# Where the stationary tiles of a two-block float32 kernel begin in SBUF

## What is computed

```python
proj = x @ w_in                                   # (256, 2048) @ (2048, ...)
merged = g_a * (o_a @ w_o_dsa) + g_b * (o_b @ w_o_moba)
x = layer_norm(ALPHA * x + merged @ w_out, ...)
x = layer_norm(ALPHA * x + mem_attention(x @ w_q, mem @ w_kv) @ w_o, ...)
g, u = jnp.split(x @ w_ffn_in, 2, axis=-1)
x = layer_norm(ALPHA * x + (silu(g) * u) @ w_ffn_out, ...)
# second block
proj = rmsnorm(x) @ w_in_2                        # three branches and their gates
y = x + sum(gates * (ys @ w_up_2)) @ w_out_2
```

## Time and profile before

| | |
|---|---|
| median of 3 runs | 2322.28 us (2319.61 to 2326.85) |
| profiled execution, span | 2323.2 us |
| PE busy | 2262.6 us, 97% |
| PEld busy (weight loads) | 1852.2 us, 80% |
| DVE busy | 1305.4 us, 56% |
| ACT busy | 1044.2 us, 45% |
| POOL busy | 167.2 us, 7% |
| read from and written to HBM | 421 MB over DMA, 181 GB/s |
| mean granted TensorE clock | 0.990 |

### The profile page before, as it was taken

One profiled execution on the slowest core, in us unless ns is written; L12 is line 12 of the kernel. 1 busy time (PEld: TensorE's weight loads), 2 busy tenths in 40 slices (PEclk: granted clock), 3 DMA queues, 4 the chain that ended last, 5 costly groups with the idle time before them and its releaser, 6 DMA issues.

```text
span 2323.2 us, 30087 instructions
## 1 busy us (share of the span) xinstructions
PE 2262.6 (97%) x10167; PEld 1852.2 (80%) x10167; DVE 1305.4 (56%) x1571; ACT 1044.2 (45%) x1243; POOL 167.2 (7%) x175
## 2 busy tenths in 40 slices
PE   7999999999999899999999999998999999999999
PEld 6777888888877678878887888776888788888887
DVE  5444655566567665445444444456655565645664
ACT  4443444555434444433444334334445444545643
POOL 1000000001204040000000000004000000200020
PEclk9999999999999999999999999998999999999999
DMA  7655554555855455555665556554556655655555
GB/s 214 205 162 155 170 169 153 180 156 180 272 195 164 156 181 187 178 187 184 195 190 181 181 181 199 176 176 137 177 167 202 191 177 185 208 176 183 175 181 164
DMA packets 216427, 421.11 MB, mean 181 GB/s; under 512 B 15225, under 2 KB 19361, under 8 KB 214433
## 3 DMA queue, kind: packets, MB, share of 16 engines
q1 hardware_dynamic: 213184, 402.31, 55.2%
q0 software_dynamic: 3168, 17.82, 2.2%
HBM read 417.97 MB, written 2.11 MB: 181 GB/s over the span
## 4 chain that ended last, share of the span: by engine, by line
PE 94%; DVE 3%; DMA 1%; ACT 1%; issue 1%; SPq 0%; DVEq 0%; ACTq 0%
PE b_ps L532 88%; PE b_ps L574 1%; PE b_ps L557 1%; PE b_ps L614 1%; DVE b_x_res L1452 1%; PE b_ps L676 1%; DVE b_w_lo L1294 1%; DVE b_x_res L1443 1%; DMA b_stage<-in_w_up 1%; PE b_ps L629 1%; DMA b_stage<-in_w_in 0%; PE b_ps L623 0%; PE b_ps L694 0%; PE b_ps L630 0%; ACT b_nat L964 0%
## 5 line engine op out<-in xcount | busy, mean ns | idle before, releaser
L1294 DVE TENSOR_TENSOR b_w_lo<-b_stage,b_w_hi 128x1024 fp32r<-128x1024 f32 (+1 forms) x762 | 930.2, 1240 | 625.8 <-ACT b_w_hi L937 620.0
L937 ACT ACTIVATE b_w_hi<-b_stage 128x1024 fp32r<-128x1024 f32 (+1 forms) x762 | 793.8, 1054 | 723.6 <-PE b_ps L532 688.9
L532 PE MATMUL b_ps<-b_w_hi,b_x_hi 128*128 128x512 f32 (+1 forms) x2368 | 944.5, 399 | 10.7 <-DVE b_x_lo L1335 8.0
L532 PE MATMUL b_ps<-b_w_hi,b_x_lo 128*128 128x512 f32 (+1 forms) x2368 | 924.7, 390 | 0.0
L532 PE MATMUL b_ps<-b_w_lo,b_x_hi 128*128 128x512 f32 (+1 forms) x2368 | 923.5, 390 | 0.0
L532 PEld LDWEIGHTS b_ps<-b_w_hi,b_x_hi 128*128 128x128 f32 x2368 | 447.6, 189 | 106.9 <-DVE b_x_lo L1335 9.2
L532 PEld LDWEIGHTS b_ps<-b_w_hi,b_x_lo 128*128 128x128 f32 x2368 | 447.0, 189 | 94.4
L532 PEld LDWEIGHTS b_ps<-b_w_lo,b_x_hi 128*128 128x128 f32 x2368 | 447.8, 189 | 88.1
L532 PE MATMUL b_ps<-b_w_hi,b_ff_h 128*128 128x512 f32 x352 | 141.3, 401 | 6.2 <-DVE b_ff_l L1335 6.2
L532 PE MATMUL b_ps<-b_w_lo,b_ff_h 128*128 128x512 f32 x352 | 140.8, 400 | 0.0
L532 PE MATMUL b_ps<-b_w_hi,b_ff_l 128*128 128x512 f32 x352 | 140.5, 399 | 0.0
(11 more groups left out here) (275 smaller groups left out, 1453.5 us busy)
## 6 DMA issues: line engine op xcount, KB each, us to landing
b_stage<-in_w_in SPq DMA_DIRECT2D x336, 512.0 KB, 4.1
b_stage<-in_w_ffn_in SPq DMA_DIRECT2D x176, 512.0 KB, 4.3
b_stage<-in_w_ffn_out SPq DMA_DIRECT2D x88, 512.0 KB, 4.2
b_stage<-in_w_out SPq DMA_DIRECT2D x64, 512.0 KB, 4.2
b_stage<-in_w_up SPq DMA_DIRECT2D x24, 512.0 KB, 3.9
b_stage<-in_w_o_dsa SPq DMA_DIRECT2D x16, 512.0 KB, 4.3
b_stage<-in_w_o_moba SPq DMA_DIRECT2D x16, 512.0 KB, 4.4
b_stage<-in_w_kv_mem SPq DMA_DIRECT2D x16, 512.0 KB, 4.1
```

Of the source, the lines that this page charges most:

```text
L532: ins = mm(ps[:, ACC + r, 0:n], x[:, kt + t, rows], w[:, slot, t, 0:n], start=first and t == 0 and k == 0, stop=last and t == GK - 1 and k ...
L937: act.activation(w_hi[:, slot, :, 0:n], stage[:, slot, :, 0:n], ACT.Copy)\
L1294: dve.tensor_tensor(w_lo[:, slot, :, 0:n], stage[:, slot, :, 0:n], w_hi[:, slot, :, 0:n].bitcast(F32), ALU.subtract).then_inc(sem("lo_done ...
```

## The change

`x_hi` and `x_lo` get rows of XP = 260 values, of which 256 are used, so that tile kt begins 16 x kt bytes past a multiple of 128 (modulo 128: eight offsets, each for two of the 16 tiles). Both tensors grow by 256 bytes, which is again a multiple of 128. A tensor `align` of 64 bytes that nothing uses is declared behind the tiny ones; with it and the 512 bytes, all tensors behind `g_col` begin at a multiple of 128, and those between `align` and `g_col` 64 bytes past one. Where x was taken with its whole rows, the slice 0:S is written out.

```diff
 SLOTS = 4
+XP = S + 4
...
-        x_hi = sb("x_hi", [P, KT, S], F32R)
-        x_lo = sb("x_lo", [P, KT, S], F32R)
+        x_hi = sb("x_hi", [P, KT, XP], F32R)
+        x_lo = sb("x_lo", [P, KT, XP], F32R)
...
         rinv = sb("rinv", [P, R])
+        sb("align", [P, 16])
...
                     for x in (x_hi, x_lo):
-                        ins = mm(ps[0:2 * H_B2, AUX, 0:S], wf2[:, kt, :], x[:, kt, :],
+                        ins = mm(ps[0:2 * H_B2, AUX, 0:S], wf2[:, kt, :], x[:, kt, 0:S],
...
                 for t in range(2):
-                    hi_batch(dst[:, 2 * t:2 * t + 2, :], t, scale)
+                    hi_batch(dst[:, 2 * t:2 * t + 2, 0:S], t, scale)
...
                     if j + 2 < KT // 2:
-                        hi_batch(dst[:, 2 * j + 4:2 * j + 6, :], j + 2, scale)
+                        hi_batch(dst[:, 2 * j + 4:2 * j + 6, 0:S], j + 2, scale)
...
                 def batch(t):
-                    lo_batch(hi[:, 2 * t:2 * t + 2, :], lo[:, 2 * t:2 * t + 2, :], t, scale)
+                    lo_batch(hi[:, 2 * t:2 * t + 2, 0:S], lo[:, 2 * t:2 * t + 2, 0:S], t, scale)
```

## The result

The changed kernel takes 2353.49 us (median of 3 runs, 2352.16 to 2353.68), the kernel before 2322.28: ratio 1.0133, 95% interval 1.0114 to 1.0151, or 26 to 35 us more. The forecast was 2338 with a range to 2354: right in sign, 15 us short, and half a microsecond inside the range's upper end. Rival (c) had 2350.

A forecast was written before the change was run, and what follows sets the result against it. PE's own rate, the spacing of L532's matmuls, was taken as the bound. +29.1 us for x less 13.6 for the other operands gave +15.5, from the 2322.3 median to 2338; own range 2328 to 2348, whole range 2285 to 2354.

The forecast's parts named there:

- Rival (c): L532's x matmuls: every offset but 0 costs like 64, +41.4 - 13.6 = +27.8 us, 2350; chance 0.11.
- part one: L532's 2040 matmuls on other stationary operands move from 64 to 0 on the 128-byte grid, 233.3 to 226.7 ns: -13.6 us.
- part two: L532's 7104 matmuls on x_hi and x_lo go from 226.7 to 230.8 ns through the staggered tiles: +29.1 us.
- What bounds the kernel: PE's own rate, busy 97% of the span; changes in the spacing of L532's matmuls go into the span one to one.
- The copies into x: ACT's and DVE's batches write two pieces of 256, still in one instruction: taken as 0, at most 7 us more.
- the middle of the offsets: L532's x matmuls: mean of the two known offsets, 230.0 ns, +23.7 us.
- the unsettled spacing: x matmuls behind a disturbed pattern take 231.4 and 231.7 ns; a shift every three matmuls may never let them settle.
- The mechanism: L532: weight loads' reads get in the moving operand's way, in a pattern shifted by the stationary address; 13.3 or 20.0 ns lost.
- (a): L532's x matmuls: stagger breaks up collisions; with half the loss gone 220.0 ns, -61 us, 2261; chance 0.17.
- (b): L532's x matmuls: only offset 64 is bad, two tiles of 16 pay +5.9 us, sum -7.7, 2314.6; chance 0.18.
- (d): L532: low address bits don't matter, or x loses just what the others win, 2322; chance 0.12.

The follow-up runs named there:

- the map: Stretches of TensorE alone, computation left out, stationary tile at one distance from w each: 226.7 ns per matmul at 0, 16, 240 bytes, up to 234.4 at 96.
- part one alone: Kernel before plus 64 bytes of padding, x as before, the other stationary operands moved by 64 bytes: 2318.65 us beside 2322.01, ratio 0.9986.
- TensorE alone: Whole computation left out, only stretches of matmuls like L532's with stationary or moving tile at set addresses, executed once: 226.7 to 234.4 ns per matmul, settled.
- the last experiment: Computation left out again, matmul stretches with other widths, element steps and changing offsets: 231.0 ns with 8 stationary columns, nothing under 226.7 at 512 moving columns.

## Why the prediction was right, and where its sum was off

The sign and the bound were forecast rightly, the number was saved by the width of the range. Of the 15.5 us that the forecast of 2338 is short, some 12 are part one's saving that didn't come and some 4 are part two's cost, and both errors go the same way. 2353.49 is above the forecast's own range of 2328 to 2348 and 0.5 us inside the whole range, whose upper end stood there for rival (c), a rule that the map disproves. That it is inside is luck: the ratio's interval, 26 to 35 us more, reaches past 2354.

**What bounds the kernel: right.** The spacing of L532's matmuls went into the time one to one: +32 us worked out from the starts, +31 measured, with waits, clock, loads and copies unchanged. The copies into x cost nothing (ACT's 596 ns for 597; DVE's batch of b_x_lo, 689 ns in both traces), as taken.

**Part one, -13.6 us: wrong, and the main miss.** The step that failed is "they move by 576 bytes, from 64 to 0 on the grid. Each goes from 233.3 to 226.7 ns". The rows had two places and one difference between them; they could not tell the stationary tile's own address from its distance to w, nor 128 bytes from 256, and the prediction took the first of each. x and w happened to share their place. What counts is the distance to w, on 256 bytes: the move took the others from distance 64 to 128, which is worth -1.4 us by the spacings and -3.4 by the run of part one alone. The spacing of 226.7 was there to be had, by 192 bytes instead of 64: both runs on w's place reached it in ff and gave some 10 us.

**Part two, +29.1 us: right in kind, small by a seventh.** Alone it measured +31.0; the spacing is 232.2 ns where 230.8 was taken. The term that was too small is the middle of the offsets: the prediction took 230.0, halfway between the two that had a price, and the mean of the sixteen distances is 231.6, since nine of them are at 233.2 to 233.3. The reason that was given, an offset that changes every three matmuls never settles, is shown by itself (231.0 ns for 240, 0, 16 in turn, each 226.7 when it stays), but in the changed kernel it accounts for no more than 232.2 - 231.6 = 0.6 ns of the 5.5. So the unsettled spacing of rows 11 and 12, 231.4 and 231.7, came nearer to the measured one mostly by coincidence.

**The mechanism** that was given, the weight loads' reads getting in the way of the moving operand's, is not shown. That it needs both operands' addresses speaks for reads that meet; that a load of 8 columns loses 231.0 - 213.3 = 17.7 ns, as much as one of 128 at a middling distance, speaks against counting the load's reads. The cause below the distance stays open.

**The rivals.** (a) fell: no offset and no changing pattern is under 226.7. (b) fell: 32, 48, 96 and 112 are as bad as 64 or worse. (c) had nearly the right time, 2350, from a wrong rule (16 and 240 cost nothing while they stay) and from a gain of 13.6 that didn't come. (d) gave 2322 and is excluded for x: one and the same tensor is at 226.7 or at 233.3 ns by its distance to w. The Trainium skill, "SBUF — State Buffer", section "Who interferes with whom", calls PE's two read ports independent and says that PE never waits on anyone; this case's traces don't agree as far as the two operands of PE itself go, since the spacing changes by 6.6 ns with the distance between them while no other engine works.

## What to carry to other kernels

Put the stationary tiles of float32r matmuls of this form (128 x 128 stationary, 512 moving columns in one piece) at the moving tiles' place on the 256-byte grid, and keep the distance the same from one matmul to the next; padding that makes it change costs nearly as much (232.2 ns) as most constant distances (233.3). For narrower stationary tiles the place has to be measured again. Where two stretches of a trace differ in a rate and in an address, list all that the addresses differ in (own place, distance, size of grid) before one of them is priced; a shift of everything by the same amount tells own place from distance in one run, and two paddings tell the size of the grid. The best version here is the kernel before with 192 or 448 bytes of padding ahead of the late tensors: 2312.2 and 2311.5 us, ratios 0.9950 and 0.9960 to before.

## What was not expected of the hardware

The spacing of a float32r matmul at the 2.4 GHz level depends on the distance of its two operands, between 226.7 and 234.4 ns for 512 columns, and repeats every 256 bytes. It settles only after several matmuls (six or seven in rows 11 and 12), and one distance has more than one settled value: at 128 the changed kernel's ff stretch ran at 232.4 ns, that of part one alone (324 matmuls from 1284.60 to 1360.20) at 233.3, and TensorE alone had 231.9, 232.5 and 233.3. Float32 matmuls of 512 columns, in the last experiment, showed none of it in the settled stretch. The 12 that are issued stand in the trace as 24, and these are 429 ns apart at distance 0 (L130) and at distance 64 (L131) alike.
